# A layer's input projection begun pair by pair while the modulation weights are still loading

## The chip, the cores and the metric

The kernel runs on one core of a Trainium2 chip. The metric is the device time of one execution in microseconds (us). The core has a TensorE (PE: matmuls and weight loads), a VectorE (DVE), a ScalarE (ACT), a GpSimd (POOL), and DMA queues that are filled here mostly by SyncE (SP).

## What is computed

One layer of a hybrid backbone over 512 latent tokens and 256 context tokens with 2048 features, in float32. Only the beginning matters here:

```
mod_x = silu(c) @ w_mod + b_mod          # six vectors of 2048: shift, scale, gate, shift, scale, gate
mod_c = silu(c_ctx) @ w_mod + b_mod      # the same for the context tokens
hx = rmsnorm(x, g_mix) * (1 + sc1) + sh1
hc = rmsnorm(ctx, g_mix) * (1 + csc1) + csh1
px = hx @ w_in                           # columns of an mLSTM and of a convolution branch
pc = hc @ w_in[:, :M_COLS]               # only the mLSTM's columns
```

Behind it come the convolution, the mLSTM, an output projection, and an expert FFN over 16384 single-neuron experts, which is most of the time.

## The kernel before

Each engine has an order of its own, written out by hand, and the engines meet at semaphores.

**Feature tiles and products.** The 2048 features are 16 tiles of 128, called `k`. Normalised tokens are transposed into `xT`, [128 features, 16 tiles, 768 tokens]; the tokens are columns 0 to 511, the context 512 to 767. A float32 product is made of three fp32r matmuls (`mm3`, line 1949 for its matmuls): each operand is split into a rounded upper part (`hT_hi`, `w_hi`, by ScalarE) and a rest (`hT_lo` by VectorE, `ring_lo` by GpSimd).

**The ring.** `ring` holds four quarters of 1 MB. Every weight block of 512 columns comes in four quarters; quarter q has the feature tiles 4q to 4q+3. SyncE loads a place as soon as TensorE (`quarter_used`) or VectorE (`row_added`) has used what stood in it.

**Modulation.** Blocks 0 to 3 of `w_mod` are the shift's 2048 columns, 4 to 7 the scale's. They come in this order. A quarter is used by four matmuls with 32 columns of weights, side by side in the array (`row_quarter`, line 1957). When a block's four quarters are through, ScalarE copies its bank (line 837), TensorE turns it into columns (`mod_columns`, line 1966), and VectorE adds the bias (line 1315). The blocks 8 to 15 of `w_mod` are summed by VectorE (`sum_rows`, lines 1355 and 1358), beside the projection.

**Tokens.** Six tiles of 128 rows (four of x, two of ctx) load between the blocks. ScalarE squares and sums them (`mean_square`, line 816), VectorE normalises (line 1302), TensorE transposes four feature tiles at a time (`turn_x`, line 1976), ScalarE copies them to `xT` (line 825).

**Projection.** `w_in` is 12 blocks of 512 columns, so 48 pieces `r` of one ring quarter each. Blocks 0 to 7 are the *sets* j: for a set, its 16 feature tiles are accumulated into the four banks 4(j%2) to 4(j%2)+3, over the 512 tokens. A piece is four feature tiles, a feature tile is 12 matmuls of 512 columns. ScalarE's `split_hi` (line 450) and GpSimd's `split_lo` (line 457) prepare a piece; ScalarE's `empty_set` (line 901) copies a finished set out. The piece two ahead is split when a piece is used. Before set 0, VectorE modulates all 16 tiles, tokens and context, and subtracts (lines 1336 and 1331), while ScalarE makes the upper parts (line 844); piece 0 is split in four steps (lines 850 and 672). Only when the last modulation block is through can the first tile be modulated, as the scale stands in blocks 4 to 7.

Pieces 32 to 47 (k and v) also use the context.

## Time and profile before

| | us |
|---|---|
| median of 3 runs | 3474.15 |
| the three runs | 3473.5, 3474.15, 3483.53 |
| profiled execution, its own time | 3474.17 |
| its span | 3472.5 |
| TensorE busy | 3391.7 (98%) |
| VectorE busy | 2218.6 (64%) |
| ScalarE busy | 1013.0 (29%) |
| GpSimd busy | 1953.0 (56%) |

The span is from the first to the last instruction on the engines; the time has 1.7 us more around it. The profile's page cuts the span into 40 slices of 86.8 us and gives a digit of busy share for each, so the stage that the change touches, up to about 161 us, is the first two slices. Whoever wants to know what happens there reads the timeline, the chain of waits and the windows.

### The profile page before, as it was taken

Reading aid. Unit: us, or ns where it says so; the run is one execution under the profiler, and the core shown is the slowest. Engines: PE = TensorE matmul, PEld = TensorE weight load, DVE = VectorE, ACT = ScalarE, POOL = GpSimd, SP = SyncE. Lnnn points to the kernel's source line nnn. Section 1 sums busy time; section 2 is a strip of 40 time slices with the busy share of each in tenths; the row PEclk is TensorE's granted clock in tenths of the full one; section 3 lists DMA queues with packets and bytes.
Section 4 is the critical chain, followed back from the end, with each engine's and each line's share of the span. In section 5 each row is a group of like instructions: output and inputs, shape, how many; then the busy total and the mean of one; then the engine's idle time right before and its main releaser. Section 6 shows DMA issues by size and latency. Waiting matters only on the chain.

```text
span 3472.5 us, 44859 instructions
## 1 busy us (share of the span) xinstructions
PE 3391.7 (98%) x17051; PEld 2937.1 (85%) x17051; DVE 2218.6 (64%) x3734; ACT 1013.0 (29%) x1150; POOL 1953.0 (56%) x938
## 2 busy tenths in 40 slices
PE   6899999999999999999999999999999999999998
PEld 2688888765788889999999999999888888888886
DVE  1546676224514568994787887864667676777666
ACT  3422211142323223223322222223233233232333
POOL 0344432211544445776666666667777777777764
PEclk7999999999999999999999999999999999999999
DMA  9556652248534226777677777778988888888872
GB/s 383 193 193 206 215 171 83 83 167 325 215 114 158 85 90 249 268 273 280 259 304 308 272 283 312 302 305 308 380 333 322 322 329 321 318 329 320 322 278 97
DMA packets 177719, 874.71 MB, mean 252 GB/s; under 512 B 15866, under 2 KB 76746, under 8 KB 88897
## 3 DMA queue, kind: packets, MB, share of 16 engines
q1 hardware_dynamic: 115248, 525.37, 41.4%
q0 software_dynamic: 38688, 281.15, 19.9%
q10 hardware_dynamic: 23664, 66.69, 5.1%
q8 instruction: 65, 1.06, 0.1%
q14 instruction: 54, 0.43, 0.0%
HBM read 803.78 MB, written 69.32 MB: 251 GB/s over the span
## 4 chain that ended last, share of the span: by engine, by line
PE 90%; DVE 5%; DMA 3%; POOL 1%; issue 1%; ACT 0%; ACTq 0%; DVEq 0%; SPq 0%; POOLq 0%
PE bank L1949 84%; DMA ring<-in_w_mod 2%; PE bank L2178 2%; PE bank L2294 1%; PE bank L2150 1%; PE bank L1957 1%; PE bank L2278 0%; DMA low<-k 0%; POOL low L714 0%; DVE low L1336 0%; DVE acc L1840 0%; DVE b L1714 0%; PE bank L2242 0%; DVE acc L1831 0%; DVE b L1694 0%
## 5 line engine op out<-in xcount | busy, mean ns | idle before, releaser
L756 POOL TENSOR_TENSOR split<-ring,split 128x1024 fp32r<-128x1024 f32 x544 | 1304.9, 2411 | 564.5 <-ACT split L1059 562.8
L1949 PE MATMUL bank<-h_hi,split 128*128 128x384 f32 (+1 forms) x4608 | 1220.1, 341 | 7.0 <-POOL split L756 5.8
L1059 ACT ACTIVATE split<-ring 128x1024 fp32r<-128x1024 f32 x544 | 577.5, 1062 | 1606.5 <-PE bank L1949 1574.4
L1949 PE MATMUL bank<-split,a_split 128*128 128x512 f32 x4608 | 1045.0, 389 | 0.1
L1949 PEld LDWEIGHTS bank<-split,a_split 128*128 128x128 f32 x4608 | 865.0, 188 | 179.8 <-POOL split L756 0.5
L1949 PEld LDWEIGHTS bank<-h_hi,split 128*128 128x128 f32 x4608 | 838.1, 188 | 27.8 <-POOL split L756 7.0
L1949 PE MATMUL bank<-h_lo,split 128*128 128x384 f32 (+1 forms) x2304 | 784.7, 341 | 0.0
L1949 PEld LDWEIGHTS bank<-h_lo,split 128*128 128x128 f32 x2304 | 433.1, 188 | 9.5
L1831 DVE TENSOR_TENSOR acc<-acc,bank 128x512 f32<-128x512 f32 x372 | 251.3, 682 | 289.8 <-PE bank L1949 288.9
L457 POOL TENSOR_TENSOR ring_lo<-ring,w_hi 128x2048 fp32r<-128x2048 f32 x47 | 219.8, 4676 | 374.6 <-ACT w_hi L450 374.6
L1949 PE MATMUL bank<-hT_hi,w_hi 128*128 128x512 f32 (+1 forms) x768 | 287.2, 374 | 6.0 <-POOL ring_lo L672 4.6
L1949 PE MATMUL bank<-hT_lo,w_hi 128*128 128x512 f32 (+1 forms) x768 | 286.7, 373 | 0.0
L1949 PE MATMUL bank<-hT_hi,ring_lo 128*128 128x512 f32 (+1 forms) x768 | 285.9, 372 | 0.0
L1395 DVE SCALAR_TENSOR_TENSOR top<-top,conv_col 128x512 f32<-128x512 f32 x240 | 161.8, 746 | 62.0 <-POOL ring_lo L457 62.0
L450 ACT ACTIVATE w_hi<-ring 128x2048 fp32r<-128x2048 f32 x47 | 90.1, 1916 | 376.3 <-PE bank L1949 373.2
L1773 DVE SCALAR_TENSOR_TENSOR onehot<-bank,expT,tiny 128x256 fp32r<-128x256 f32 x384 | 180.5, 470 | 0.0
L1949 PEld LDWEIGHTS bank<-hT_hi,w_hi 128*128 128x128 f32 x768 | 145.0, 189 | 34.6 <-issue 8.0
L1785 DVE TENSOR_REDUCE b<-bank 128x512 f32<-128x1024 f32 x96 | 116.7, 1216 | 87.1 <-PE bank L2294 87.1
L1949 PEld LDWEIGHTS bank<-hT_hi,ring_lo 128*128 128x128 f32 x768 | 144.8, 188 | 25.9
L1949 PEld LDWEIGHTS bank<-hT_lo,w_hi 128*128 128x128 f32 x768 | 145.1, 189 | 25.2
L1358 DVE SCALAR_TENSOR_TENSOR bank<-ring,c_silu,bank 128x512 f32<-128x512 f32 x120 | 90.7, 756 | 69.1 <-ACT w_hi L450 48.5
L1771 DVE TENSOR_SCALAR onehot<-bank,expT 128x128 fp32r<-128x128 f32 x384 | 129.6, 337 | 0.0
(296 smaller groups left out, 3609.1 us busy)
## 6 DMA issues: line engine op xcount, KB each, us to landing
ring<-in_u_emb SPq DMA_DIRECT2D x128, 1024.0 KB
ring<-in_v_emb SPq DMA_DIRECT2D x128, 1024.0 KB
ring<-in_w_mod SPq DMA_DIRECT2D x64, 1024.0 KB
ring<-in_w_in SPq DMA_DIRECT2D x48, 1024.0 KB
ring<-in_w_mod SPq DMA_DIRECT2D x64, 512.0 KB, 4.6
neurons<-tiny ACTq DMA_DIRECT2D x128, 192.0 KB
gate_table<-b ACTq DMA_DIRECT2D x6, 4096.0 KB, 14.8
weigh<-neurons SPq DMA_DIRECT2D x32, 768.0 KB
```

Of the source, the lines that this page charges most:

```text
L450: nc.scalar.activation(weight_slot(r).bitcast(F32R), ring[:, at, :, :].rearrange("p k n -> p (k n)"), ACT.Copy).then_inc(whi_made, 1)
L457: nc.gpsimd.tensor_tensor(ring_lo[:, at, :].bitcast(F32R), ring[:, at, :, :].rearrange("p k n -> p (k n)"), weight_slot(r), op=ALU.subtrac ...
L756: nc.gpsimd.tensor_tensor(split[:, r % 2, 1, at].bitcast(F32R), ring[:, r % 4, :, :].rearrange("p k n -> p (k n)")[:, at], split[:, r % 2, ...
L1059: nc.scalar.activation(split[:, q % 2, 0, at].bitcast(F32R), ring[:, q, :, :].rearrange("p k n -> p (k n)")[:, at], ACT.Copy)\
L1358: nc.vector.scalar_tensor_tensor(rows, ring[:, 3, kk, :], factor, rows, ALU.mult, ALU.add)\
L1395: nc.vector.scalar_tensor_tensor(y, u, w, y, ALU.mult, ALU.add).then_inc(conv_step, 1)
L1771: nc.vector.tensor_scalar(onehot[:, grp % 2, s, 0, :].bitcast(F32R), iota_bank, expT[:, 1, tok], None, ALU.is_equal)
L1773: last = nc.vector.scalar_tensor_tensor(onehot[:, grp % 2, s, 1:3, :].bitcast(F32R), iota_bank.unsqueeze(1).to_broadcast([P, 2, P]), expT[ ...
L1785: nc.vector.tensor_reduce(stage[:, :, at:at + 4].rearrange("p i t -> p t i"), parts, AX.X, ALU.add)\
L1831: nc.vector.tensor_tensor(part, part, src, ALU.add).then_inc(sum_free, 1)
L1949: last = mm(out_, left[a].bitcast(F32R), right[b].bitcast(F32R), start=start and n == 0, stop=stop and n == 2)
L2178: last = mm(bank[:, 4 + n % 2, 0:HD + 1], probT[:, d, s, j * P:(j + 1) * P], v_aug[:, s, h, :], start=i == 0, stop=i == len(keys) - 1)
```

## The change

**Blocks in pairs.** The order of modulation blocks is now 0, 4, 1, 5, 2, 6, 3, 7 (`mod_block`). After blocks 0 and 4 the shift and scale of feature tiles 0 to 3 are known, and so on.

**Projection amid the loads.** Set 0 (pieces 0 to 3) goes to banks 0 to 3. Piece p has the feature tiles of pair p; its four steps (`first_piece`, 12 matmuls each) stand behind quarters 2, 4, 6 and 7 of every eight, one pair later. The last two steps of piece 2 and all of piece 3 stand behind the last quarter. The pieces 0 to 3 load to places of their own (`first_w`, two of 1 MB in `top`, with `first_lo` for their rests), between the blocks.

**Tokens and context.** The four token tiles load right behind block 0 and are all transposed amid block 1. The context tiles load behind the last modulation quarter and piece 4. They are transposed by TensorE in pieces 4 and 5, one group of four ahead of each feature tile; VectorE modulates them after its second row sum, and subtracts after the fifth; ScalarE makes the upper parts at pieces 6 to 9. The context uses banks 0 to 2, so its first transpose waits until set 0 is emptied.

**Bookkeeping.** The transposes now use banks 0 to 3, modulation rows 4 and 5, columns 6 and 7; pieces from 4 on take ring places 0 to 2 in another phase, so the counts of loads per place differ (`MOD2`, `WO`, `WQ`).

The core of the diff:

```diff
+def mod_block(i):
+    return i // 2 + 4 * (i % 2)
+def row_used(n):
+    return n + 1 + max(0, n // 8 - 1)
...
 # SyncE
+            for i in range(8):
                 for q in range(4):
+                    if i:
+                        sp.wait_ge(quarter_used, row_used(4 * i + q - 4))
+                    load(q, part(w_mod, mod_block(i), q))
+                if i == 0:
+                    for t in range(LT):
+                        x_load(t)
+                if i % 2 == 0:
+                    first_load(i // 2)
...
+            in_load(4)
+            for i in range(LT, LT + CT):
+                sp.wait_ge(tr_full, 4 * LT)
+                x_load(i)
+            in_load(5)
+            in_load(6)
             row_halves(0)
-            for r in range(3, 7):
-                in_load(r)
...
 # ScalarE
+            rows_copied(0)
+            for i in range(LT):
+                mean_square(i)
+            for i in range(LT):
                 for g in range(4):
+                    transposed(i, g)
+            split_hi(act, 0)
+            rows_copied(1)
+            for p in range(4):
+                for k in range(4 * p, 4 * p + 4):
+                    token_hi(k)
+                if p < 3:
+                    rows_copied(2 * p + 2)
+                    split_hi(act, p + 1)
+                    rows_copied(2 * p + 3)
+            mean_square(LT)
+            mean_square(LT + 1)
...
                     r = 4 * j + q
+                    if r < 2:
+                        continue
+                    if r in (4, 5):
+                        for n in range(4):
+                            transposed(LT + r - 4, n)
                     act.wait_ge(quarter_used, weights_used(r))
+                    split_hi(act, r + 2)
+                    if 6 <= r < 10:
+                        for k in range(4 * r - 24, 4 * r - 20):
+                            context_hi(k)
...
 # VectorE
+            for i in range(8):
+                b = mod_block(i)
+                dve.wait_ge(mod_summed, i + 1)
...
+                for k in range(4 * p, 4 * p + 4):
+                    modulate(k, 0, slice(0, T))
+                    if k % 4:
+                        rest1(k - 1, slice(0, T), k)
+                rest1(4 * p + 3, slice(0, T), 4 * p + 4)
+            for i in range(LT, LT + CT):
+                normalise(i)
...
             for r in range(CONV_TURN - 5):
                 sum_rows(r)
+                if r == 1:
+                    dve.wait_ge(tr_free, 4 * (LT + CT))
+                    for k in range(KT):
+                        modulate(k, 1, slice(T, L))
+                if r == 4:
+                    for k in range(KT):
+                        rest1(k, slice(T, L), KT + k + 1)
...
 # TensorE
+            for n in range(32):
+                i, q = n // 4, n % 4
+                pe.wait_ge(quarter_full[q], 16 * (i + 1))
+                row_quarter(4 + i % 2, q, q)
+                if n == 4:
+                    setup_columns()
+                if i and q == 0:
+                    mod_columns(i - 1)
+                if i == 1:
+                    for g in range(4):
+                        turn_x(q, g)
+                if n >= 8 and n % 8 in (2, 4, 6, 7) and not (n == 30 or n == 31):
+                    first_piece(n // 8 - 1, (2, 4, 6, 7).index(n % 8))
+            first_piece(2, 2, (0, 1))
+            mod_columns(7)
+            first_piece(2, 2, (2, 3))
+            first_piece(2, 3)
+            for kk in range(QT):
+                first_piece(3, kk)
...
-            for j in range(PAIRED):
+            for j in range(1, PAIRED):
...
+                        if r in (4, 5):
+                            pe.wait_ge(set_free, 3)
+                            turn_x(r, kk)
+                        if r == 8 and kk == 0:
+                            pe.wait_ge(tr_free, 4 * (LT + CT))
```

**How instructions moved.** TensorE before, at the end of the modulation blocks: the last transposes (L1976), the last quarter (L1957), the column product (L1966), and only then the projection (L1949).

```order
L1976 MATMUL bank<-ident,top 128x128 [waits tr_free,h_made]
L1976 MATMUL bank<-ident,top 128x128 x3
L1957 MATMUL bank<-ring,c_rep 32x512 [waits quarter_full3]
L1957 MATMUL bank<-ring,c_rep 32x512 x3
L1966 MATMUL bank<-low 128x2 [waits mod_bank_free,row_copied]
L1966 MATMUL bank<-low 128x2 x3
L1949 MATMUL bank<-hT_hi,w_hi 128x512 [waits first_split,h_split,set_free,mod_bank_free]
L1949 MATMUL bank<-hT_lo,w_hi 128x512
```

TensorE after the change, behind quarter 8 (L2006 is a quarter, L2017 the column product, L1998 a projection matmul): the first step of piece 0 stands behind quarter 10, of 32.

```order
L2006 MATMUL bank<-ring,c_rep 32x512 [waits quarter_full0]
L2006 MATMUL bank<-ring,c_rep 32x512 x3
L2017 MATMUL bank<-gate_w,low 128x2 [waits dve_a,mod_bank_free,row_copied]
L2017 MATMUL bank<-gate_w,low 128x2 x3
L2006 MATMUL bank<-ring,c_rep 32x512 [waits quarter_full1]
L2006 MATMUL bank<-ring,c_rep 32x512 x3
L2006 MATMUL bank<-ring,c_rep 32x512 [waits quarter_full2]
L2006 MATMUL bank<-ring,c_rep 32x512 x3
L1998 MATMUL bank<-hT_hi,w_hi 128x512 [waits h_split,wsplit_made]
L1998 MATMUL bank<-hT_lo,w_hi 128x512
L1998 MATMUL bank<-hT_hi,first_lo 128x512
```

So 40 of the 64 tile products of set 0 (ten steps of four) now stand ahead of the last quarter, where none did.

ScalarE after the change, between the last token upper parts (L862) and piece 6: the context squares (L843), then the splits of pieces 4 and 5 (L480), the emptying of set 0 (L928), and copies of context transposes (L852) around the split of piece 6.

```order
L862 ACTIVATE hT_hi<-low 128x512 [waits modulated1] x4
L843 ACTIVATE top,stat<-top 128x2048 [waits x_squared,x_loaded4]
L846 ACTIVATE stat<-stat,eps_col 128x1 [waits x_squared]
L843 ACTIVATE top,stat<-top 128x2048 [waits x_squared,x_loaded5]
L846 ACTIVATE stat<-stat,eps_col 128x1 [waits x_squared]
...
L480 ACTIVATE w_hi<-ring 128x2048 [waits quarter_used,quarter_full1]
L480 ACTIVATE w_hi<-ring 128x2048 [waits quarter_used,quarter_full2]
L928 ACTIVATE top<-bank 128x2048
L852 ACTIVATE low<-bank 128x4x128 [waits tr_full] x4
L480 ACTIVATE w_hi<-ring 128x2048 [waits quarter_used,quarter_full0]
L852 ACTIVATE low<-bank 128x4x128 [waits tr_full] x4
```

Before, the squares stood amid the modulation blocks, and TensorE's piece 4 did not depend on L928.

## Rows read from the trace of the kernel before

**Rows 1.** The page: busy time, and TensorE in 40 slices, with its clock.

```profile
PE 3391.7 (98%) x17051; PEld 2937.1 (85%) x17051; DVE 2218.6 (64%) x3734; ACT 1013.0 (29%) x1150; POOL 1953.0 (56%) x938
PE   6899999999999999999999999999999999999998
PEclk7999999999999999999999999999999999999999
```

**Rows 2.** Chain of waits, from the start to 700 us: start us, us, what.

```profile
105.84 1.11 PE bank L1957 x8
106.97 0.61 ACT low L837
107.62 1.58 PE bank L1966 x8
...
121.31 5.07 DVE low L1336 x2
138.82 207.06 PE bank L1949 x912
```

**Rows 3.** TensorE's timeline: start us, us, engine, line, operation, out<-in, count.

```profile
26.66 1.93 PE L1957 MATMUL bank<-ring,c_rep 128*32 128x512 f32 x8 [10.47 <-DMA ring<-in_w_mod]
...
77.25 1.94 PE L1957 MATMUL bank<-ring,c_rep 128*32 128x512 f32 x8 [3.33 <-DMA ring<-in_w_mod]
...
86.06 1.06 PE L1957 MATMUL bank<-ring,c_rep 128*32 128x512 f32 x8
87.05 0.66 PE L1976 MATMUL bank<-ident,top 128*128 128x128 f32 x4
87.64 1.06 PE L1957 MATMUL bank<-ring,c_rep 128*32 128x512 f32 x8
88.88 1.05 PE L1966 MATMUL bank<-low 128*128 128x2 f32 x8 [0.18 <-ACT low L837]
89.80 0.63 PE L1976 MATMUL bank<-ident,top 128*128 128x128 f32 x4
...
113.77 0.77 PE L1949 MATMUL bank<-hT_hi,w_hi 128*128 128x512 f32 x1 [4.59 <-POOL ring_lo L672]
```

**Rows 4.** ScalarE's timeline.

```profile
36.89 0.60 ACT L837 ACTIVATE low<-bank 128x512 f32<-128x512 f32 x1 [11.03 <-PE bank L1957]
...
161.03 1.92 ACT L450 ACTIVATE w_hi<-ring 128x2048 fp32r<-128x2048 f32 x1 [5.33 <-PE bank L1949]
162.86 1.86 ACT L901 ACTIVATE top<-bank 128x2048 f32<-128x2048 f32 x1
171.91 1.92 ACT L450 ACTIVATE w_hi<-ring 128x2048 fp32r<-128x2048 f32 x1 [7.20 <-PE bank L1949]
```

**Rows 5.** Windows: engines' busy us, then granted clock, DMA share, GB/s.

```profile
0.00:20.00 20.00, 6.38 (x33) 1.25 (x33) 0.75 (x4) 2.83 (x4) 1.90 (x13) 0.90 0.92 357
20.00:40.00 20.00, 10.63 (x54) 4.40 (x58) 4.00 (x11) 7.91 (x11) 0.00 (x0) 0.59 0.94 372
...
64.00:72.00 8.00, 7.22 (x44) 3.00 (x44) 1.52 (x3) 3.31 (x5) 0.00 (x0) 0.79 1.01 419
88.00:96.00 8.00, 5.61 (x48) 2.59 (x44) 0.17 (x1) 2.62 (x5) 0.00 (x0) 1.00 1.00 385
96.00:104.00 8.00, 6.76 (x56) 3.08 (x52) 0.17 (x1) 2.77 (x5) 0.00 (x0) 1.00 1.01 422
```

**Rows 6.** Timelines of VectorE and, last row, of GpSimd.

```profile
121.23 5.15 DVE L1336 TENSOR_SCALAR low<-low,soft 128x512 f32<-128x512 f32 x2
127.17 0.86 DVE L1336 TENSOR_SCALAR low<-low,soft 128x512 f32<-128x512 f32 x2
189.35 3.20 DVE L1358 SCALAR_TENSOR_TENSOR bank<-ring,c_silu,bank 128x512 f32<-128x512 f32 x4 [7.70 <-DMA ring<-in_w_mod]
121.56 4.67 POOL L457 TENSOR_TENSOR ring_lo<-ring,w_hi 128x2048 fp32r<-128x2048 f32 x1 [3.37 <-ACT w_hi L450]
```

**Rows 7.** DMA issues up to 200 us: size, us to landing.

```profile
ring<-in_w_mod SPq DMA_DIRECT2D x10, 512.0 KB, 6.3
```

More of the change, by code:

```diff
@@ L162, in hybrid_layer @@
             m_split = region("m_split", T, heads)[:, :]
+        with ExitStack() as begin:
+            region("begin_place", 28696 + 8192, begin)
+            first_lo = region("first_lo", 4096, begin)[:, :].rearrange("p (s w) -> p s w", s=2)
         with ExitStack() as project:
@@ L207, in hybrid_layer @@
         ring = R0.rearrange("p (q k n) -> p q k n", q=4, n=NB)
-        x_slot = [top[:, i * D:(i + 1) * D] for i in range(6)]
+        x_slot = [top[:, i * D:(i + 1) * D] for i in (0, 1, 2, 3, 2, 3)]
+        first_w = top[:, 8192:12288].rearrange("p (s w) -> p s w", s=2)
         vec_rows = low[0:32, 0:P]
@@ L316, in hybrid_layer @@
         whi_made = sem("whi_made")
-        first_hi = sem("first_hi")
-        first_split = sem("first_split")
+        first_full = [sem(f"first_full{s}") for s in range(2)]
         wsplit_made = sem("wsplit_made")
@@ L483, in weight_load @@
                 load(ring_place(r)[0], src)
-            for q in range(4):
-                load(q, part(w_mod, 0, q))
             def x_load(i):
@@ L490, in x_load, with first_load @@
                 sp.dma_start(x_slot[i], src).then_inc(x_loaded[i], 16)
-            x_load(0)
-            x_load(1)
-            for b in range(1, 8):
-                for q in range(4):
-                    sp.wait_ge(quarter_used, b * 4 + (q - 3))
-                    load(q, part(w_mod, b, q))
-                if b <= 4:
-                    x_load(b + 1)
+            def first_load(r):
+                if r >= 2:
+                    sp.wait_ge(quarter_used, weights_used(r - 2))
+                sp.dma_start(first_w[:, r % 2, :], w_in[0, r, :, :]).then_inc(first_full[r % 2], 16)
+            for i in range(8):
+                for q in range(4):
+                    if i:
[6 more added lines that the diff above has]
+                    first_load(i // 2)
             def in_load(r):
@@ L677, in glu_product @@
                                         op=ALU.mult).then_inc(glu_used, 1)
-            for r in range(1, WO_R):
+            for r in range(WO_R):
                 split_lo(pool, r)
+                if r == 6:
+                    pool.wait_ge(x_squared, LT + CT)
+                    nc.gpsimd.memset(top[:, 0:4 * UPW], 0.0).then_inc(consts_made, 1)
                 if r == 9:
@@ L1087, in square2 @@
                                      accum_out=hssq[:, 4 * j + b:4 * j + b + 1]).then_inc(x2_squared, 1)
-            landed = 16 * WQ
+            landed = [16 * n for n in WQ]
             for r in range(WO_R + 2, WO_R + 15):
@@ L1978, in turn_x, with weight_parts @@
                 last.then_inc(tr_full, 1)
[L1981 to L1994 removed]
+            def weight_parts(r, kk, at):
+                cols = slice(kk * NB + at.start, kk * NB + at.stop)
+                return [weight_slot(r)[:, cols], weight_rest(r)[:, cols]]
@@ new lines, in h_parts, with first_piece @@
+            def h_parts(k, at):
+                return [hT_hi[:, k, at], hT_lo[:, k, at]]
+            def first_piece(r, kk, tiles=range(4)):
+                k = r * QT + kk
+                pe.wait_ge(wsplit_made, r + 1)
+                pe.wait_ge(h_split, k + 1)
+                for m in tiles:
+                    last = mm3(bank[:, m, :], weight_parts(r, kk, slice(m * P, (m + 1) * P)), h_parts(k, slice(0, T)),
+                               k == 0, k == KT - 1)
+                if kk == QT - 1 and 3 in tiles:
+                    last.then_inc(quarter_used, 1)
```

236 lines of the change are left out of this document (96 added, 140 removed).

## The prediction

> **What bounds the kernel now.** I read the page first: TensorE is busy for 98% of the span, and of 40 slices only the first shows it idle for a third of the time and below full clock [rows 1]. So a change to the start is worth what it takes off the time at which TensorE's unbroken work begins, and not more. Next I read the chain of waits from 80 us on [rows 2]. Up to 105.8 us it runs through the DMA of modulation weights into the ring, each quarter followed by 1 us of matmuls; then through the last block's chain (row copy, column matmuls, adds); then through VectorE's modulation and split of the 16 feature tiles, in which one pair of instructions stands at 5.1 us; from 138.8 us on it is TensorE alone, 912 matmuls in 207.1 us, 0.227 us each. In TensorE's timeline [rows 3] the last quarter's matmuls begin at 105.84 and the first projection matmul at 113.77. The end of the first projection set is read off ScalarE, which splits piece 5 when TensorE has used piece 3: 161.03 us, and piece 6 when it has used piece 4: 171.91 [rows 4]. One piece is 48 matmuls, 10.9 us, and the first four pieces take 161.0 - 113.8 = 47.2 us, of which 43.5 is matmul time and 3.7 waiting and half clock.
>
> Set 1 (pieces 4 to 7) therefore starts at 161.0 now. All behind it is the same work in the same order, bound by TensorE, so the forecast is a new time for that start.
>
> **The change, part by part.**
>
> (1) The loads. Before the last modulation quarter there were 38 loads of 1 MB (32 modulation quarters, 6 token and context tiles); now there are 40 (32, 4 token tiles, 4 pieces of w_in). From 64 us on the ring ran at 419 to 422 GB/s [rows 5], 2.5 us a load. Two more loads move the last quarter from 105.84 to 110.9 us, if DMA still sets the pace.
>
> (2) TensorE amid the loads. Quarter 4 is now the tenth load instead of the seventh: it was used at 26.66 us [rows 3]. In strict order that is 7.5 us later, 34.2; but transfers were visibly in flight side by side in the first 27 us (357 GB/s for 20 us and 372 for the next 6.7 [rows 5] are 9.6 MB, some 9.2 loads' worth, while 7 had landed), which puts the lower end at 28. I take 31. From there to the start of the last quarter TensorE has, at full clock: 27 quarters at 0.99 us (the distance from 86.06 to 87.05), the setup columns 1.5, 7 column products at 0.92 (88.88 to 89.80), 16 groups of four token transposes at 0.59 (87.05 to 87.64), and ten projection steps of 12 matmuls at 0.227, 2.72 each: 26.7 + 1.5 + 6.4 + 9.4 + 27.2 = 71.2 us. [Rows 3] carry the first four, [rows 2] the fifth.
>
> Two waits are new in this queue. Column product 1 waits for a ScalarE queue in which 16 copies, the split of piece 0 (1.9 us) and a row copy stand ahead of it: about 2 us beyond the quarter that covers it. And step 0 of the first pair waits for adds, modulation (about 0.5 us for 512 columns), ScalarE's copy and VectorE's subtraction. That chain alone is 2.1 us (0.4, 0.5, 0.6, 0.6), but GpSimd's split of piece 0 falls on it. In the rows, while GpSimd's 4.67 us split runs from 121.56, VectorE's two modulations take 5.15 us from 121.23 on, against 0.86 for the same pair at 127.17 [rows 6]. I add 3 us. The Trainium skill, in "SBUF — State Buffer", section on the ports, says that VectorE in its two-port modes and GpSimd take the shared port pair in turns, each for a whole instruction. The trace agrees, with that 5.15 beside 0.86.
>
> The clock: quarters run at 1.06 us at 2.4 GHz and 1.94 at 1.2 GHz. After a gap of 3.3 us TensorE ran from 77.25 to about 84.5 at the half clock, which cost half of 7.2, 3.6 us; after gaps under 1.6 us, from 87 on, it kept the full clock [rows 3, 5]. Three gaps of two or more microseconds remain (before quarter 4, and the two waits): 3.6 + 2.2 + 2.2 = 8 us.
>
> The last quarter then starts at 31 + 71.2 + 5 + 8 = 115.2 us. That is behind the DMA's 110.9: the loads are no longer the bound of this stage, TensorE's queue is, and the loads wait for ring places.
>
> (3) From the last quarter to set 1. Quarter 1.0, half a step 1.4, column product 0.9, half a step 1.4, step 11 2.7, and the four steps of the last pair 10.9: 18.3 us, to 133.5. The last block's chain (row copy 0.6 [rows 4], adds, modulation, copy, subtraction, 3 us in all) is hidden by the 4.1 us of matmuls between its column product and step 12; without that cover it would cost 3.
>
> (4) A stall before piece 4. Its first instruction is now a context transpose, which waits for ScalarE to have emptied set 0. ScalarE begins with piece 5's split once piece 3 is used, then copies the banks: 1.92 + 1.86 as at 161.03 and 162.86 [rows 4], 3.8 us. Before, piece 4 waited for neither. Piece 4's own split comes after the two context tiles' squares, which need their loads, third and fourth behind the last modulation quarter; I have it done within 2 us of the same time, so it adds nothing. 133.5 + 3.8 = 137.3.
>
> (5) Context transposes. Eight groups of four, formerly covered by DMA waits, now stand between the matmuls of pieces 4 and 5: 8 x 0.59 = 4.7 us. The 3.8 us gap ahead of them costs a half-clock spell as at 77.25: 3.6 us.
>
> (6) Context modulation and subtraction: 32 VectorE operations, under 0.5 us each, beside set 1. ScalarE's take of the summed rows at piece 6 needs four row sums, the third of which is now behind 16 modulations. With 3.2 us a sum [rows 6] and 6.3 us for a half load to land [rows 7], that sum comes some 7 us later than piece 6's end, but ScalarE is next needed at the end of piece 7, 10.9 us on. Nothing. The order of ring places and the counters cost nothing: the same number of loads and waits.
>
> **Sum.** Set 1, counted without its additions, starts at 137.3 + 4.7 + 3.6 = 145.6 instead of 161.0: 15.4 us. The profiled execution took 3474.17, the median 3474.15. Forecast 3459 us.
>
> The bounds: quarter 4 at 28 or 34 (-3, +3); the half clock from 0 to 16 us in (2) (-8, +8); the two waits 0 to 9 (-5, +4); the stall 0 (if ScalarE were there at once) to 8, with the late context loads (-4, +4); the spell in (5) none or as counted (-4, 0). They won't all fall on one side; together some -9 and +8.
>
> **The rivals.** What a measurement of this kernel can tell from no change is about 0.3%, 10.4 us, so the line lies at 3463.7.
>
> A: *the loads are the bound and the rest is covered.* If TensorE stays at full clock and the waits are short, the last quarter is at 110.9, the stall and its spell stay. Gain 15.4 + 4.3 = 19.7, and without the last spell 23: 3451 to 3454. For it: the clock granted was 1.00 from 88 to 104 us [rows 5]. Against: the backlog begins with 16 transpose groups before the first pair.
>
> B: *given back at the seam.* Context tiles load late, piece 4's split is late behind their squares, row sums late behind modulation; each 2 to 4 us on ScalarE's queue. Gain 5 to 9: 3465 to 3469, within 0.3%. For it: ScalarE and VectorE have more queued at the seam than in any stretch before. Against: piece 6 and 7 leave 10.9 us each.
>
> C: *the port lock.* By the rule of (2), GpSimd's split of each next piece may meet each pair's modulation, four times up to 4.2 us (5.1 - 0.9), 16.8, of which 3 is in my sum: 3473, no change. Against: the split is queued behind the even block's row copy and the modulation behind the odd block's, four quarters apart, some 10 us against 4.67.
>
> D, slower: *half clock through the load stage.* The 71.2 us of (2) take about 66 more at the half clock (1.94 against 1.06 for a quarter, and matmuls twice as long). The gain is gone when the half clock holds for 31 us beyond the 16 counted; were it to hold for all of the stage the time would be 3459 + 58 = 3517, for two thirds of it some 3490. For it: 0.59 was granted from 20 to 40 us and 0.79 from 64 to 72 [rows 5]. Against: those stretches had DMA gaps of 2 to 10 us, which the backlog fills.
>
> That the change doesn't do what it says (the steps stand in the queue but all wait) would show as DMA share falling in the load stage; its price is that of C.
>
> **Chances.** Forecast 0.62, with a range of its own of 3451 to 3463; A 0.10; B 0.20; C 0.03; D 0.05. Faster by over 0.3%: 0.62 + 0.10 = 0.72. Within 0.3%: B and C, 0.23. Slower: D, 0.05. The range of 8 in 10 takes A's better half and nearly all of B: 3450 to 3469.
>
> **What would show it.** Last quarter's matmuls at 113 to 118 us with DMA share below 0.95 before them; step 12 without a wait; a gap of about 4 us before the first context transpose, released by ScalarE's emptying of set 0; piece 5 used at about 167.4, and from there pieces 10.9 us apart. Wrong would be a gap before piece 8 or 9, a half clock for more than 20 us between 35 and 110, or piece 5 used after 172.

## The result, and the profile after

| | before | after |
|---|---|---|
| median, us | 3476.28 (20 runs, 3471.28 to 3485.95) | 3483.43 (20 runs, 3478.5 to 3488.8) |
| ratio | 1 | 1.0019, 95% interval 1.0012 to 1.0026 |
| profiled execution, its time and span | 3474.17, 3472.5 | 3479.79, 3477.9 |

The change makes the kernel slower, by 7.2 us between the medians and 6.6 by the ratio. That is within the 0.3% the prediction counts as no change, and far outside its range of 3450 to 3469. Whole-kernel busy time hides where it went. The page of after, against [rows 1]: busy times, then the chain by engine, then by line.

```profile
PE 3385.9 (97%) x17051; PEld 2935.1 (84%) x17051; DVE 2319.3 (67%) x3753; ACT 1013.5 (29%) x1163; POOL 1953.6 (56%) x935
PE 82%; DVE 12%; DMA 2%; issue 2%; POOL 1%; ACT 1%; ACTq 0%; DVEq 0%; SPq 0%; POOLq 0%
PE bank L1998 76%; DVE top L1444 5%; PE bank L2244 2%; DVE bank L1400 2%; DMA ring<-in_w_mod 2%; PE bank L2360 1%; PE bank L2216 1%; PE bank L2006 1%; DMA low<-k 0%; PE bank L2344 0%; POOL low L741 0%; DVE acc L1889 0%; DVE b L1763 0%; PE bank L2030 0%; PE bank L2308 0%
```

TensorE has slightly less busy time, but VectorE has 101 us more (2319.3 against 2218.6) from 19 more instructions, and it stands on the chain for 12% of the span, where it was 5%. L1444 is a step of the convolution, L1400 a row sum. The change does not touch either.

**The start went nearly as forecast.** The chain of waits of after, start us, us, what:

```profile
34.02 1.93 PE bank L2006 x8
...
55.60 2.81 DVE soft L1370
...
79.15 8.12 DMA ring<-in_w_mod
87.31 1.06 PE bank L2006 x8
...
109.63 9.00 DMA ring<-in_w_mod
118.68 1.06 PE bank L2006 x8
...
137.68 1.91 ACT w_hi L480
139.59 1.77 ACT top L928
141.72 1.09 PE bank L2030 x4
...
166.07 46.30 PE bank L1998 x204
212.48 1.92 ACT w_hi L480
```

Quarter 4 is used at 34.02, the last quarter at 118.68 (105.84 in [rows 2]), set 0 is done at 137.68, and the first context transpose starts at 141.72 after a wait of 4.16 us on ScalarE's emptying.

**The lead, piece by piece.** When piece r is used, ScalarE begins the split of piece r + 2. Where it has waited for nothing but TensorE, that start is a clock of TensorE, and only such starts are in the table (after against the first profile of before, minus is earlier):

| piece used | 3 | 5 | 9 | 12 | 14 | 16 | 20 | 24 | 28 | 45 |
|---|---|---|---|---|---|---|---|---|---|---|
| before, us | 161.03 | 182.79 | 226.31 | 258.95 | 280.71 | 302.47 | 345.99 | 390.74 | 434.26 | 720.73 |
| after, us | 137.68 | 168.96 | 212.48 | 252.70 | 274.46 | 297.97 | 343.29 | 388.89 | 434.36 | 721.62 |
| lead, us | -23.4 | -13.8 | -13.8 | -6.2 | -6.2 | -4.5 | -2.7 | -1.9 | +0.1 | +0.9 |

So 13.8 us were won and held to 212. Of these 7.6 were lost at one point, ahead of and in piece 12, and the rest in small portions, nearly all of it by 434.

**The one point.** VectorE's timeline of after (start us, us, engine, line, operation, out<-in, count, idle before and releaser):

```profile
197.88 2.41 DVE L1400 SCALAR_TENSOR_TENSOR bank<-ring,c_silu,bank 128x512 f32<-128x512 f32 x3
200.19 10.59 DVE L1355 TENSOR_TENSOR hT_lo<-low,hT_hi 128x256 fp32r<-128x256 f32 x12
214.73 5.63 DVE L1355 TENSOR_TENSOR hT_lo<-low,hT_hi 128x256 fp32r<-128x256 f32 x4 [3.94 <-ACT hT_hi L866]
220.29 3.19 DVE L1400 SCALAR_TENSOR_TENSOR bank<-ring,c_silu,bank 128x512 f32<-128x512 f32 x4
```

The 16 context subtractions stand in a block between the fifth and the sixth row sum. They last from 200.2 to 220.3: 3.9 us waiting for ScalarE's last upper parts, which by the change's own order come only at piece 9, and 16.2 us of work, 1.0 us each. The sixth sum, which frees two ring halves, starts at 220.29; before, it started at 217.44. What follows, on SyncE's queue, ScalarE and TensorE of after:

```profile
221.85 1.98 SPq L546 DMA_DIRECT2D ring<-in_w_mod  x2
223.87 0.43 SPq L500 DMA_DIRECT2D ring<-in_w_in  x1
232.37 1.92 ACT L480 ACTIVATE w_hi<-ring 128x2048 fp32r<-128x2048 f32 x1 [16.75 <-DMA ring<-in_w_in]
239.21 0.76 PE L1998 MATMUL bank<-hT_hi,w_hi 128*128 128x512 f32 x1 [5.09 <-POOL ring_lo L485]
```

The load of the piece is queued on SyncE behind the row halves that this sum frees. TensorE had gained 13.8 us and so wanted the piece 13.8 us sooner, while VectorE released its ring places no sooner than before. TensorE stood still for 5.1 us here; behind the gap its granted clock was 0.69 from 239.2 to 246 us, which makes up the rest of the 7.6.

**The small portions.** VectorE of before, in two turns (L1358 is the row sum, L1395 the convolution's steps), then GpSimd's splits of weights:

```profile
228.26 3.19 DVE L1358 SCALAR_TENSOR_TENSOR bank<-ring,c_silu,bank 128x512 f32<-128x512 f32 x4 [2.54 <-ACT w_hi L450]
232.96 4.06 DVE L1395 SCALAR_TENSOR_TENSOR top<-top,conv_col 128x512 f32<-128x512 f32 x6 [1.50 <-POOL ring_lo L457]
239.14 3.19 DVE L1358 SCALAR_TENSOR_TENSOR bank<-ring,c_silu,bank 128x512 f32<-128x512 f32 x4 [2.12 <-ACT w_hi L450]
...
228.31 4.61 POOL L457 TENSOR_TENSOR ring_lo<-ring,w_hi 128x2048 fp32r<-128x2048 f32 x1 [6.27 <-ACT w_hi L450]
239.19 4.61 POOL L457 TENSOR_TENSOR ring_lo<-ring,w_hi 128x2048 fp32r<-128x2048 f32 x1 [6.27 <-ACT w_hi L450]
```

The same of after:

```profile
254.08 8.42 DVE L1444 SCALAR_TENSOR_TENSOR top<-top,conv_col 128x512 f32<-128x512 f32 x6
262.42 3.19 DVE L1400 SCALAR_TENSOR_TENSOR bank<-ring,c_silu,bank 128x512 f32<-128x512 f32 x4
265.51 8.41 DVE L1444 SCALAR_TENSOR_TENSOR top<-top,conv_col 128x512 f32<-128x512 f32 x6
273.84 3.19 DVE L1400 SCALAR_TENSOR_TENSOR bank<-ring,c_silu,bank 128x512 f32<-128x512 f32 x4
...
254.69 4.60 POOL L485 TENSOR_TENSOR ring_lo<-ring,w_hi 128x2048 fp32r<-128x2048 f32 x1 [4.85 <-ACT w_hi L480]
265.57 5.14 POOL L485 TENSOR_TENSOR ring_lo<-ring,w_hi 128x2048 fp32r<-128x2048 f32 x1 [6.28 <-ACT w_hi L480]
```

Before, a turn is a row sum beside GpSimd's split (228.26 and 228.31), then the convolution behind it (it waits 1.5 us for the split), then 2.1 us of rest: 10.88 us, TensorE's pace of a piece. The sum takes 3.19 us although GpSimd is at work, so these two don't disturb each other; one of its operands is in a bank. In after the convolution falls on the split: six steps take 8.42 us instead of 4.06, the 4.4 us more being nearly one GpSimd split, and a turn is 262.42 to 273.84, 11.42 us. That is longer than TensorE's 10.88. VectorE no longer rests and falls behind TensorE by half a microsecond a turn. Since GpSimd's split starts when the ring's next piece has come, which VectorE's sum releases, the two stay together. Nothing in the loop parts them. From piece 32 on a turn has 14 steps and they still collide (13.73 us instead of 9.37), but TensorE's pieces there last 16.8 us, and the lead changes by only 0.8 us more. The Trainium skill, "SBUF — State Buffer", section on the two separate sides, says that a VectorE instruction with two SBUF inputs and a GpSimd one that reads SBUF exclude each other for a whole instruction. The rows agree, as to both the convolution (both operands in SBUF) and the sum.

VectorE's lateness reaches TensorE once in four pieces. A block's row sum stands in a bank that TensorE needs for its next set, so ScalarE copies the sum out first. Before, that copy is done 5 us ahead of TensorE's next use (first two rows); in after it waits 11.69 us for VectorE's sum, and TensorE waits for the copy (last two rows):

```profile
285.90 0.60 ACT L870 ACTIVATE top<-bank 128x512 f32<-128x512 f32 x1 [3.27 <-DVE bank L1358]
291.59 1.92 ACT L450 ACTIVATE w_hi<-ring 128x2048 fp32r<-128x2048 f32 x1 [5.10 <-PE bank L1949]
...
288.06 0.60 ACT L897 ACTIVATE top<-bank 128x512 f32<-128x512 f32 x1 [11.69 <-DVE bank L1400]
288.71 0.50 PE L1998 MATMUL bank<-hT_hi,w_hi 128*128 128x512 f32 x1 [1.45 <-ACT top L897]
```

The same wait is 1.50 us at 334.03, 0.19 at 379.64 and 1.65 at 425.11.

The groups of VectorE from 200 to 540 us, busy and mean ns of one, idle before it and releasers; first of before, then of after:

```profile
L1395 DVE SCALAR_TENSOR_TENSOR top<-top,conv_col 128x512 f32<-128x512 f32 x187 | 126.4, 746 | 29.7 <-POOL ring_lo L457 29.7
L1358 DVE SCALAR_TENSOR_TENSOR bank<-ring,c_silu,bank 128x512 f32<-128x512 f32 x105 | 79.3, 756 | 53.4 <-ACT w_hi L450 48.5
```

```profile
L1444 DVE SCALAR_TENSOR_TENSOR top<-top,conv_col 128x512 f32<-128x512 f32 x183 | 218.3, 1260 | 0.0
L1400 DVE SCALAR_TENSOR_TENSOR bank<-ring,c_silu,bank 128x512 f32<-128x512 f32 x103 | 77.6, 753 | 9.7 <-DMA ring<-in_w_mod 4.8 <-issue 0.3
```

VectorE's rest of 83 us has gone into the convolution's steps, of which one takes 1260 ns instead of 746; the sums are unchanged.

### The profile page after: what moved, and what is told of

It is laid out like the page before. It is cut to its first block, busy times and chain, and to the rows that moved or that the text cites. A ratio compares the mean times of both kernels' runs of the same rounds, so it can differ in the third digit from the quotient of the medians.

```text
span 3477.9 us, 44897 instructions
## 1 busy us (share of the span) xinstructions
PE 3385.9 (97%) x17051; PEld 2935.1 (84%) x17051; DVE 2319.3 (67%) x3753; ACT 1013.5 (29%) x1163; POOL 1953.6 (56%) x935
## 4 chain that ended last, share of the span: by engine, by line
PE 82%; DVE 12%; DMA 2%; issue 2%; POOL 1%; ACT 1%; ACTq 0%; DVEq 0%; SPq 0%; POOLq 0%
PE bank L1998 76%; DVE top L1444 5%; PE bank L2244 2%; DVE bank L1400 2%; DMA ring<-in_w_mod 2%; PE bank L2360 1%; PE bank L2216 1%; PE bank L2006 1%; DMA low<-k 0%; PE bank L2344 0%; POOL low L741 0%; DVE acc L1889 0%; DVE b L1763 0%; PE bank L2030 0%; PE bank L2308 0%
## 5 line engine op out<-in xcount | busy, mean ns | idle before, releaser
L1998 PE MATMUL bank<-h_hi,split 128*128 128x384 f32 (+1 forms) x4608 | 1220.2, 341 | 6.9 <-POOL split L783 5.8
L1998 PE MATMUL bank<-split,a_split 128*128 128x512 f32 x4608 | 1045.0, 389 | 0.1
L1998 PEld LDWEIGHTS bank<-split,a_split 128*128 128x128 f32 x4608 | 864.8, 188 | 180.0 <-POOL split L783 0.5
L1998 PEld LDWEIGHTS bank<-h_hi,split 128*128 128x128 f32 x4608 | 838.7, 188 | 27.7 <-POOL split L783 6.9
L1998 PE MATMUL bank<-h_lo,split 128*128 128x384 f32 (+1 forms) x2304 | 784.7, 341 | 0.0
L1998 PEld LDWEIGHTS bank<-h_lo,split 128*128 128x128 f32 x2304 | 433.2, 188 | 9.5
L485 POOL TENSOR_TENSOR ring_lo<-ring,w_hi 128x2048 fp32r<-128x2048 f32 x44 | 209.9, 4769 | 370.5 <-ACT w_hi L480 370.2
L1998 PE MATMUL bank<-hT_hi,w_hi 128*128 128x512 f32 (+1 forms) x768 | 290.2, 378 | 15.1 <-POOL ring_lo L485 5.4
L1998 PE MATMUL bank<-hT_lo,w_hi 128*128 128x512 f32 (+1 forms) x768 | 287.4, 374 | 0.0
L1444 DVE SCALAR_TENSOR_TENSOR top<-top,conv_col 128x512 f32<-128x512 f32 x240 | 256.4, 1138 | 22.9 <-POOL ring_lo L485 22.9
L1998 PE MATMUL bank<-hT_hi,ring_lo 128*128 128x512 f32 (+1 forms) x704 | 261.4, 371 | 0.0
L1998 PEld LDWEIGHTS bank<-hT_hi,w_hi 128*128 128x128 f32 x768 | 145.2, 189 | 52.8 <-issue 18.2
L480 ACT ACTIVATE w_hi<-ring 128x2048 fp32r<-128x2048 f32 x44 | 84.3, 1917 | 321.1 <-PE bank L1998 273.1
L1998 PEld LDWEIGHTS bank<-hT_lo,w_hi 128*128 128x128 f32 x768 | 145.3, 189 | 24.7
L1998 PEld LDWEIGHTS bank<-hT_hi,ring_lo 128*128 128x128 f32 x704 | 133.0, 189 | 23.5
L1702 DVE CUSTOM_DVE_ANT_0 rows_b<-bank,rows_b 128x1920 f32<-128x1920 f32 x43 | 92.4, 2150 | 42.6 <-DMA rows_b<-in_u_rows,small 42.3
```

The costliest lines, as they stand in the source:

```text
L480: nc.scalar.activation(weight_slot(r).bitcast(F32R), weight_words(r), ACT.Copy).then_inc(whi_made, 1)
L485: nc.gpsimd.tensor_tensor(weight_rest(r).bitcast(F32R), weight_words(r), weight_slot(r), op=ALU.subtract).then_inc(wsplit_made, 1)
L1444: nc.vector.scalar_tensor_tensor(y, u, w, y, ALU.mult, ALU.add).then_inc(conv_step, 1)
L1702: last = nc.vector.tensor_tensor_reduce(out=rows, in0=h2_rows, in1=rows, scale=1.0, scalar=0.0, op0=ALU.mult, op1=ALU.add, accum_out=sums[ ...
L1998: last = mm(out_, left[a].bitcast(F32R), right[b].bitcast(F32R), start=start and n == 0, stop=stop and n == 2)
```

## The experiments

**Theory 1**: the context subtractions make VectorE's sixth sum late against TensorE's demand (one loss), and from there the convolution stays on GpSimd's splits (the small losses). "The lock" below is this: the two meeting turn after turn. Its rivals are named in each text. All leads below are of the profiled execution against the first profile of before, at piece 45's use (the row 720.73), minus for earlier; the times are medians beside runs of before on the same chip (3475.57 for the first four experiments, 3477.06 for the next four).

**e1: the block spread.** From the changed kernel.

```diff
-                if r == 4:
-                    for k in range(KT):
-                        rest1(k, slice(T, L), KT + k + 1)
...
+                if t < CONV_TURN + KT:
+                    k = t - CONV_TURN
+                    rest1(k, slice(T, L), KT + k + 1)
```

> Takes the 16 context subtractions of VectorE out of one block after the fifth row sum and puts one into each of the 16 conv turns from piece 10 on. Theory 1 (the block of subtractions makes VectorE a turn late, and from then on its convolution steps meet GpSimd's splits on the shared port, 11.4 us a turn against 10.88 a piece): pieces stay 10.88 us apart through piece 36, the convolution step is back at about 0.75 us, and the time is 3462 to 3468, some 14 us under the changed kernel. Theory 2 (the lead is lost to the later weight loads on SyncE's queue or to ScalarE's context work, whatever VectorE does): 3478 to 3484. A third, that the end of the paired pieces is bound by VectorE's total work: 3470 to 3476, with the lead shrinking evenly.

Measured: 3470.97 us, ratio 0.998 (0.997 to 0.999). The lead is 11.8 us at every piece from 5 to 45. A subtraction costs 0.42 us, and the convolution is back behind the split:

```profile
227.36 3.20 DVE L1400 SCALAR_TENSOR_TENSOR bank<-ring,c_silu,bank 128x512 f32<-128x512 f32 x4 [1.78 <-ACT w_hi L480]
232.05 0.43 DVE L1355 TENSOR_TENSOR hT_lo<-low,hT_hi 128x256 fp32r<-128x256 f32 x1 [1.49 <-POOL ring_lo L485]
232.40 4.06 DVE L1444 SCALAR_TENSOR_TENSOR top<-top,conv_col 128x512 f32<-128x512 f32 x6
```

And its group of steps on the page (busy us, mean ns of one):

```profile
L1444 DVE SCALAR_TENSOR_TENSOR top<-top,conv_col 128x512 f32<-128x512 f32 x240 | 161.8, 746 | 45.6 <-POOL ring_lo L485 45.6
```

The same sixteen operations, at another place, cost nothing up to piece 45. VectorE's sixth sum, at 217.44 in before, starts here at

```profile
205.66 1.55 DVE L1400 SCALAR_TENSOR_TENSOR bank<-ring,c_silu,bank 128x512 f32<-128x512 f32 x2 [3.32 <-ACT w_hi L480]
```

which is 11.8 us earlier: without the block VectorE moves forward with TensorE, and the rest around this sum (3.32, 0.56 and 0.97 us, then 2.25 to GpSimd's next split) is still 7.1 us. The loads, their order and TensorE's queue are those of the changed kernel, so these aren't the cause of the loss. The median, however, lies above Theory 1's 3462 to 3468 and in the range of the third theory, whose evenly shrinking lead isn't there; what is lost on the way to the end lies behind piece 45 (below, with r3).

**e2: only the one loss made small.** From the changed kernel: ScalarE makes the upper parts at pieces 6 and 7, so the block need not wait.

```diff
-                    if 6 <= r < 10:
-                        for k in range(4 * r - 24, 4 * r - 20):
+                    if 6 <= r < 8:
+                        for k in range(8 * r - 48, 8 * r - 40):
```

> ScalarE makes the 16 context upper parts at pieces 6 and 7 (eight each) instead of 6 to 9 (four each); VectorE's block of 16 subtractions stays where it is but no longer waits 3.9 us for them. Theory 1 splits its cost in two: the one-time late load of piece 12 (9 us) should vanish, since the block ends at about 211 us, while VectorE is still one turn late and keeps meeting GpSimd: 0.5 us a piece over some 20 pieces. That gives 3472 to 3477, with a convolution step still near 1.1 us. If the 9 us alone were the cause the time would be 3470 to 3474 with the step at 0.75 us; if the wait has no part in it, 3482 to 3485.

Measured: 3478.49 us, ratio 1.0006 (0.9997 to 1.0015). The block is 11.82 us (203.76 to 215.58). The lead, 11.5 us up to piece 9, is 9.7 at piece 12, 7.9 at 16, 6.2 at 20, 5.3 at 24 and 3.6 from 28 on. TensorE's only wait on the way to piece 12 is 1.53 us for ScalarE's copy of the row sum, none for the ring. So the loss at the one point is gone, and the lock alone costs 7.9 us. The time is 1.5 us above what Theory 1 gave, and not clear of no change.

**e3: the late sixth sum, without the change.** From the kernel before: 28 memsets of 0.66 us, 18.3 us in a row, on a tile that is filled later; nothing that is computed changes.

```diff
             for r in range(CONV_TURN - 5):
                 sum_rows(r)
+            for n in range(DELAY):
+                dve.wait_ge(late, n)
+                nc.vector.memset(gate_split, 0.0).then_inc(late, 1)
+            dve.wait_ge(late, DELAY)
```

> The kernel before, with 28 idle memsets of 512 columns on VectorE (8 to 16 us in a row) between its fifth and sixth row sum, so that VectorE enters the convolution a turn late. It adds some 10 us to an engine that is 64% busy. Theory 1: the kernel before falls into the same pattern, turns of 11.4 us and a convolution step near 1.1 us, and is 8 to 20 us slower, though nothing of the change is in it. Theory 2 or 3: slower by 0 to 3 us, since VectorE has 3.6 us of slack in each piece and makes it up in four pieces.

Measured: 3489.23 us, ratio 1.004 (1.0025 to 1.0054). The profiled start was 1.3 us early; at piece 12 it is 4.1 late (TensorE waited 3.0 us for a late ring piece and 0.7 for the row copy), at the end 10.8. The kernel before shows the changed kernel's convolution:

```profile
253.06 8.43 DVE L1401 SCALAR_TENSOR_TENSOR top<-top,conv_col 128x512 f32<-128x512 f32 x6
```

```profile
L1401 DVE SCALAR_TENSOR_TENSOR top<-top,conv_col 128x512 f32<-128x512 f32 x240 | 256.2, 1138 | 22.9 <-POOL ring_lo L459 22.9
```

1138 ns is the changed kernel's mean over all 240 steps too. So a pause of VectorE at this place is sufficient.

**e4: spread, and the seam mended.** e1, and in pieces 4 and 5 the context's transposes stand behind a feature tile's matmuls instead of ahead of them, so that TensorE doesn't wait for ScalarE's emptying at once; piece 4's split goes ahead of the context squares.

```diff
-                        if r in (4, 5):
-                            pe.wait_ge(set_free, 3)
-                            turn_x(r, kk)
...
                             last = mm3(bank[:, 4 * par + m, :], weight_parts(r, kk, slice(m * P, (m + 1) * P)),
                                        h_parts(k, slice(0, T)), k == 0, k == KT - 1)
-                            last.then_inc(quarter_used, 1)
+                        if kk == QT - 1:
+                            last.then_inc(quarter_used, 1)
+                        if r in (4, 5):
+                            pe.wait_ge(set_free, 3)
+                            turn_x(r, kk)
...
+            split_hi(act, 4)
             mean_square(LT)
             mean_square(LT + 1)
...
-                    split_hi(act, r + 2)
+                    if r > 2:
+                        split_hi(act, r + 2)
```

> e1 and two changes at the seam: the context transposes stand behind each tile's projection matmuls of pieces 4 and 5 instead of ahead of them, so that piece 4 does not wait for set 0 to be emptied, and ScalarE splits piece 4 before it squares the context tiles. The stall of 3.8 us before the first transpose and the half-clock spell behind it should go, and no new one come in, as piece 4's split ends at about 134 us: 4 to 7 us under e1, 3457 to 3463. If the stall only moves (to the first transpose, behind tile 1) the gain is 0 to 2 us.

Measured: 3461.73 us, ratio 0.9965 (0.9952 to 0.9978), lead 17.3. The wait at the seam fell from 4.16 to 1.11 us, and the half clock behind it went with it (granted 1.00 from 142 to 150 us; 0.50 from 142 to 144 in after):

```profile
142.19 0.66 PE L2032 MATMUL bank<-ident,top 128*128 128x128 f32 x4 [1.11 <-ACT top L929]
```

The first transposes take 0.66 us here and 1.09 in after. In all five profiled executions with the wait of 4.16 us (after, r2, e1, e2, r3) the granted clock fell to 0.50 for some two microseconds behind it (142 to 147 us); in e4 and r4 it stayed at 1.00.

**e5: piece 0's split earlier.** e4, with ScalarE's split of piece 0 ahead of the 16 transposed copies.

```diff
                 mean_square(i)
+            split_hi(act, 0)
             for i in range(LT):
                 for g in range(4):
                     transposed(i, g)
-            split_hi(act, 0)
             rows_copied(1)
```

> e4 with ScalarE's split of piece 0 ahead of the 16 copies of token transposes instead of behind them. In the changed kernel TensorE waited 2.1 us for the row copy behind that split, and VectorE's first scale instruction took 2.8 us against 0.19 before, beside GpSimd's split of piece 0. If TensorE's queue bounds the load stage, as forecast, both go and the last quarter starts 3 to 5 us earlier: 3456 to 3461, 3 us under e4. If the loads bound it (TensorE waited 0.7 and 1.3 us for quarters near the end) the last quarter moves by under 1.5 us and the time is e4's within 2 us.

Measured: 3463.49 us, ratio 0.9959 (0.9945 to 0.9973). The last quarter moved from 119.45 to 115.72 and the lead from 17.3 to 21.1, but the time is e4's: what is won here is lost behind piece 45. Neither expectation held whole, as the first had the time lower and the second the last quarter still. GpSimd's split of piece 0 now stands at 33.92 us, and VectorE's L1370 (here L1372) takes 0.17 us.

**e6: the control.** The kernel before with the same 28 memsets, two in each of 14 turns.

```diff
+                if t < CONV_TURN + DELAY // 2:
+                    for m in range(2 * (t - CONV_TURN), 2 * (t - CONV_TURN) + 2):
+                        dve.wait_ge(late, m)
+                        nc.vector.memset(gate_split, 0.0).then_inc(late, 1)
```

> A control for e3: the kernel before with the same 28 memsets on VectorE, but two in each of 14 conv turns behind that turn's wait for GpSimd's split, not 28 in a row ahead of the first. The work added to VectorE is the same, 18 us with its waits. Theory 1 (lateness, not work): no change, 3474 to 3478, the convolution step at 0.75 us. If VectorE's load were the cause: 8 to 14 us slower, as e3 was.

Measured: 3476.82 us, ratio 0.9999 (0.9989 to 1.0008), a convolution step 740 ns. The amount of work added is not what costs; its being in one block is.

**e7 and e8: how much delay it takes.** e3 with 10 and with 16 memsets (6.6 and 10.5 us).

```diff
-DELAY = 28
+DELAY = 10
```

> e3 with 10 memsets in place of 28, 6.6 us in a row. In the kernel before, VectorE has some 4.5 us idle ahead of its sixth row sum, 1.4 between the sum and the first conv turn, and 2.2 between that turn's last step and GpSimd's next split: 8.1 us. Under that the pattern should not be entered: 3474 to 3478, step at 0.75 us. If every delay were passed on, 3 us slower.

> e3 with 16 memsets, 10.5 us in a row, past the 8.1 us: the last steps of the first conv turn meet GpSimd's next split, and the pattern should hold from there, turns of 11.4 us. No weight load comes late at the start as it did in e3 (5.6 us there), so 5 to 11 us slower than before: 3480 to 3487, with a step near 1.1 us. If the pattern needed a whole turn of delay: as e7.

Measured: 10 memsets 3476.7 us, ratio 0.9999 (0.999 to 1.0008), a step 747 ns; 16 memsets 3482.91 us, ratio 1.0015 (1.0006 to 1.0024), a step 1086 ns, and the start, 1.9 us early, ends 6.2 late. At piece 12 it is still 1.9 early, so this is the lock alone: 8.1 us. The point can be read off VectorE of before around the sixth sum:

```profile
217.44 3.20 DVE L1358 SCALAR_TENSOR_TENSOR bank<-ring,c_silu,bank 128x512 f32<-128x512 f32 x4 [4.54 <-ACT w_hi L450]
222.08 1.00 DVE L1391 TENSOR_SCALAR top<-top,conv_col,chan_col 128x512 f32<-128x512 f32 x2 [1.44 <-POOL ring_lo L457]
223.00 2.73 DVE L1395 SCALAR_TENSOR_TENSOR top<-top,conv_col 128x512 f32<-128x512 f32 x4
```

It rests 4.54 us ahead of the sum, 1.44 ahead of the convolution and 2.6 behind it, to GpSimd's next split at 228.31: together 8.6 us. With 6.6 us the first convolution ends before GpSimd's next split; with 10.5 us it doesn't (the first row is e7's, the others e8's and its GpSimd's):

```profile
222.59 2.73 DVE L1401 SCALAR_TENSOR_TENSOR top<-top,conv_col 128x512 f32<-128x512 f32 x4
```

```profile
225.55 7.08 DVE L1401 SCALAR_TENSOR_TENSOR top<-top,conv_col 128x512 f32<-128x512 f32 x4
235.65 8.41 DVE L1401 SCALAR_TENSOR_TENSOR top<-top,conv_col 128x512 f32<-128x512 f32 x6
...
226.45 4.97 POOL L459 TENSOR_TENSOR ring_lo<-ring,w_hi 128x2048 fp32r<-128x2048 f32 x1 [6.26 <-ACT w_hi L452]
```

**r1 to r4: what happens behind piece 45.** Four kernels run once more, unedited: before, after, e1 and e4. Theory C is that each execution loses there what its half-clock spells happen to cost, Theory S that the changed kernel and those made from it lose more there by their build.

> The kernel before once more, for a second profile. What is open: in the medians the kernels made from the changed one lie 3.5 to 7.5 us later than their lead at piece 47 says, those made from the kernel before only -0.4 to 2.9 us. Theory C (chance): behind piece 47 each execution draws its own half-clock spells, so this profile loses anything from 0 to 5 us against the first one behind 740 us. Theory S (systematic): the stage behind piece 47 costs some 5 us more in the changed kernel's family; this profile then loses 0 to 3 us there, as the first one and the ones with memsets did (0, 1.8, 2.6, 3.1, 3.2).

> The changed kernel once more. Up to piece 47 both theories expect the same as in its first profile: conv steps at 1138 ns, lead -4.8 at piece 12, +0.9 at piece 47. Behind it, against the first profile of the kernel before: Theory C 0 to 5 us, Theory S 4.5 to 11 us (first profiles of its family: 4.1, 4.4, 7.5, 11.2, 11.3).

> The kernel with the context subtractions spread over sixteen turns once more: lead 11.8 at piece 47 again. Behind it Theory C 0 to 5 us, Theory S 4.5 to 11; in the first profile it was 11.3, so by Theory C this one should end at 3463 to 3468 us, by Theory S at 3467 to 3474.

> The best kernel so far once more: lead 17.3 at piece 47 again, time 3459 to 3466 us by either theory; behind piece 47 Theory C 0 to 5 us lost, Theory S 4 us or more (first profile 4.1). Its ratio to the kernel before should fall in 0.9952 to 0.9978.

Measured: 3476.35 (ratio 1.0, 0.9991 to 1.0009), 3484.47 (1.0019, 1.001 to 1.0028), 3467.18 (0.9974, 0.9965 to 0.9983), 3461.43 us (0.9957, 0.9943 to 0.9971), beside 3477.1 for before. Lost behind piece 45, against the first profile of before: r1 3.2, r2 2.0, r3 6.8, r4 4.1 us. With the earlier ones that is 1.8 to 3.2 for kernels made from before (e3, e6, e7, e8, r1), 2.0 and 4.4 for the changed kernel, and 4.1 to 11.3 (e1) for those that keep a lead (e1, e2, e4, e5, r3, r4). r2's 2.0 contradicts Theory S for the changed kernel; the 6.8 of r3 lies above what Theory C allowed. So the changed kernel loses little there, and the kernels with a lead give back some 4 to 11 us of it. r2 also shows how the start varies: one step of TensorE at the half clock at 60 us (granted 0.50), 5.46 us where after's first profile has 3.03 (granted 1.00; both in the chain of waits), and its lead was 10.5 instead of 13.8, its end 4.1 late instead of 0.9.

```profile
60.64 5.46 PE bank L1998 x12
```

Where the time behind piece 45 goes is seen in part; some of it is the clock. TensorE of before, then of after, at one group of matmuls there:

```profile
780.34 10.58 PE L2150 MATMUL bank<-low 128*128 128x512 f32 x24
```

```profile
781.56 12.85 PE L2216 MATMUL bank<-low 128*128 128x512 f32 x24 [1.67 <-DMA low<-k]
```

The same 24 matmuls take 10.58 or 12.85 us, at a granted clock of 0.98 (780 to 791) and 0.79 (780 to 795). In e1 they take 13.54 at 0.78, and e1 also waits 2.2 us for GpSimd at 1495, where before has no wait. Why such spells and waits fall more often on kernels with a lead, no run tells; it stays open.

## Why the prediction was wrong

**Steps (2) to (5) held in what they name, with sizes that partly cancel, and step (6) failed.** By the terms:

| step | forecast, us | measured, us |
|---|---|---|
| quarter 4 used | 31 (28 to 34) | 34.02 |
| TensorE's waits from there to the last quarter | 5 | 8.5 (2.13, 1.97, 0.67, 0.70, 0.67, 1.00, 1.31) |
| half clock in that stretch | 8 | about 5 (the remainder: 84.7 - 71.2 - 8.5) |
| last quarter | 115.2 | 118.68 |
| from there to set 1 | 18.3 | 137.68 - 118.68 = 19.0 |
| stall at the seam | 3.8 | 4.16 |
| transposes and half clock in pieces 4 and 5 | 8.3 | 168.96 - 141.72 - 21.8 = 5.5 |
| piece 5 used | 167.4 | 168.96 |

Piece 5 is used 13.8 us earlier than before, where 15.4 was forecast. That this is only 1.6 us off is in part luck: the start and the waits were sized 6 us too low, the half clock 3 and the last term 3 too high. The two new waits, sized 5 us together, are 2.13 (column product 1 on ScalarE) and 1.97 us (step 0, behind VectorE's L1370, which took 2.80 beside GpSimd's split and 0.17 without it in e5). Three more waits, 3.0 us together, are for loads, which step (2) had off the path. In the chain of after a load stands between two quarters for 8.12 and 9.00 us: a ring place that TensorE had freed wasn't full again when TensorE came back to it. Rival A fell with the last quarter at 118.68, rival D with a granted clock of 1.00 from 64 to 120 us of after. Rival B, given back at the seam, fell too; the seam cost what was forecast.

None of the signs given for being wrong came: the gap ahead of piece 12 lies behind "a gap before piece 8 or 9". By the prediction's own line the result is "within 0.3%", which had 0.23, but neither B nor C as told there is what happened.

**The step that failed** is (6): "Context modulation and subtraction: 32 VectorE operations, under 0.5 us each, beside set 1 ... Nothing." It failed thrice. The price: a subtraction took 1.0 us in the block, with GpSimd's splits amid it, not under 0.5; one that meets no split takes 0.42 (e1). A modulation took 0.61. The margin: the step looked at the row sums at the stage's start and at ScalarE's next use, and did not ask when VectorE is needed next as the releaser of ring places. That margin is the rest around the sixth sum: 8.6 us in before (e7 and e8 lie on its two sides) and 7.1 in e1 with a lead of 11.8, so the lead itself takes little of it. The block needs 20 us, of which 3.9 are a wait that the change's own order on ScalarE makes. And the order of engines behind it: a delay of VectorE was reckoned as a delay that is caught up, while it changed what runs beside what.

The port lock was in the prediction, as rival C, but only in the load stage, where TensorE waited 1.97 us for it; the sum has 3. The other pairs' waits for VectorE were 0.67 us or none. Its place was the convolution, which the text doesn't mention, because VectorE is not on the chain of before there [rows 2]. Step (6) should have asked, for each stage that VectorE's block can shift, with what its instructions then collide.

The sum that would have been right up to piece 45: 13.8 won, 7.6 lost at the point, 7.1 lost in the small portions (from 6.2 early to 0.9 late), so 0.9 late. Of the 7.1, 6.3 are gone by piece 28, in the waits for the row copy; the last 0.8 were not traced. e1 shows the first number without the other two, e2 and e8 the lock without the point's loss (7.9 and 8.1), and e3 both without the change. The step looked at ScalarE's take of the row sums at piece 6 only; at pieces 12, 16, 20 and so on the same take is how VectorE's lateness comes to TensorE. What leads from 0.9 late to the medians' 7.2 is of the size of the scatter between executions (start 3.3 us, behind piece 45 2.0 to 4.4); it was not attributed further.

The chances: "slower" had 0.05, all of it for the half clock, which did not come. The slower rival was sought among mechanisms of the stage that the change edits, and the true one lay in the stage behind it.

**The better version.** e4 beats both kernels: 0.9965 and, run again, 0.9957 of before, some 12 to 16 us. That is close to the 15.4 that the prediction expected of the change itself, by other terms: a lead of 17.3 us at piece 45, of which some 4 are given back.

## What to carry to other kernels

When an engine off the chain gets a block of work, compare the block with that engine's rest up to its next release of a buffer, in units of time, and count in it what the block waits for and what it collides with. Where VectorE and GpSimd alternate in a loop, note which instructions run beside GpSimd's (those with an operand in a bank did, at no cost) and which behind it; a single delay that swaps them can hold for hundreds of microseconds if the swapped turn is longer than the consumer's. Spread added operations one per turn: here the same sixteen cost 16.2 us of VectorE in a block and 0.42 us each, within the rest, when spread.

## What the runs showed of the hardware

- The collision persists by itself. Once met, VectorE's convolution and GpSimd's split met in every turn (turn about 11.4 us against 10.88 up to 455 us, and still at 517, where TensorE's pieces of 16.8 us cover it). A delay of 6.6 us left no trace and one of 10.5 us cost 8.1 us up to piece 45.
- An instruction of VectorE on 8 columns (L1370) took 2.80 us behind a GpSimd instruction of 4.52 us that had begun ahead of it, and 0.17 us in e5, where that instruction stood 20 us earlier.
- The half clock differs between executions: one step of 12 took 3.03 us (granted 1.00) and 5.46 us (0.50) in two executions of the same kernel, and the same 24 matmuls took 10.58, 12.85 and 13.54 us in three kernels (0.98, 0.79, 0.78). For differences of a few microseconds, a lead read piece by piece up to such a spell is worth more than one profile's total.
